# A mixer and expert kernel on one core: down weights in 8 KB pieces, rows scattered by index, gate and up biases on VectorE

## What is computed

```python
def moe(h, w_router, b_router, w_gu, b_gu, w_down, b_down):
    logits = (xt @ w_router + b_router).astype(jnp.float32)
    top_vals, top_idx = lax.top_k(logits, TOP_K)            # 4 of 32
    weights = jax.nn.softmax(top_vals, axis=-1)
    ...
    def expert_block(args):
        xblk, e = args
        gu = xblk @ w_gu[e] + b_gu[e]                       # 1024 -> 2048
        gate, up = jnp.split(gu, 2, axis=-1)
        gate = jnp.minimum(gate, SWIGLU_LIMIT)              # 7
        up = jnp.clip(up, -SWIGLU_LIMIT, SWIGLU_LIMIT)
        act = (up + 1.0) * gate * jax.nn.sigmoid(SWIGLU_ALPHA * gate)
        return act @ w_down[e] + b_down[e]                  # 1024 -> 1024
    ...
    y = jnp.zeros((n_tok + 1, D_MODEL), yb.dtype).at[buf_tok].add(yb * buf_w[:, None])
```

## Time and profile before

| what | value |
|---|---|
| median of 3 runs | 2313.23 us (2310.96 to 2314.2) |
| the profiled execution | 2310.52 us, of which the span (first to last instruction) is 2308.7 us |
| granted TensorE clock, mean | 0.984 |
| busy: PE, DVE, ACT, POOL | 2204.4 us (95%), 795.9 us (34%), 473.4 us (21%), 155.8 us (7%) |
| moved by DMA | 557.15 MB in 145856 packets, mean 241 GB/s |
| of which q1 (issued by SP), q0 (POOL), q10 (ACT) | 513.33 MB, 30.31 MB, 12.67 MB |

### The profile page before, as it was taken

The page is one execution under the profiler, slowest core; times in us unless marked ns, Lnnn a source line. Parts: engine busy times, 40 slices in busy tenths (PEclk is TensorE's granted clock), DMA queues, the critical chain, the costliest instruction groups (busy, mean ns, idle before and its releaser), DMA issues. The chain is left out here.

```text
span 2308.7 us, 35748 instructions
## 1 busy us (share of the span) xinstructions
PE 2204.4 (95%) x14480; PEld 906.0 (39%) x14480; DVE 795.9 (34%) x1427; ACT 473.4 (21%) x848; POOL 155.8 (7%) x186
## 2 busy tenths in 40 slices
PE   5999887999999999999999995999999998999998
PEld 2434442333333333333333334455445444444443
DVE  1132447522222222222222643003176013466543
ACT  2121223111101111011110103010135002545630
POOL 0000002100111001111012311000000000000000
PEclk9999898999999999999999997999999999999999
DMA  9138529999999999999999994121210221122100
GB/s 369 56 114 310 203 107 349 415 417 417 417 416 416 416 417 417 415 416 416 415 417 415 414 406 177 64 73 66 74 54 1 73 73 62 38 91 91 73 37 37
DMA packets 145856, 557.15 MB, mean 241 GB/s; under 512 B 21125, under 2 KB 36654, under 8 KB 111906
## 3 DMA queue, kind: packets, MB, share of 16 engines
q1 hardware_dynamic: 119190, 513.33, 56.1%
q0 software_dynamic: 13200, 30.31, 3.5%
q10 hardware_dynamic: 13404, 12.67, 1.6%
HBM read 545.87 MB, written 25.03 MB: 247 GB/s over the span
## 5 line engine op out<-in xcount | busy, mean ns | idle before, releaser
L1978 PE MATMUL ps<-ring,xeT 128*32 128x512 f32 x6144 | 668.9, 594 | 0.9 <-DVE mT L1768 0.7
L1978 PEld LDWEIGHTS ps<-ring,xeT 128*32 128x32 f32 x6144 | 195.6, 110 | 446.5 <-issue 436.4
L1948 PE MATMUL ps<-ring,mT 128*32 128x512 f32 x2048 | 266.5, 592 | 0.3 <-DMA ring<-in_w_down 0.2
L1701 ACT ACTIVATE mT<-mT 128x768 f32<-128x768 f32 x32 | 27.0, 843 | 867.8 <-DVE mT L1765 867.8
L1765 DVE TENSOR_SCALAR mT<-ps 128x768 f32<-128x768 f32 x32 | 30.6, 958 | 479.9 <-PE ps L1978 479.9
L360 PE MATMUL ps<-hT_late,ring 128*128 128x512 f32 x384 | 165.2, 592 | 1.1 <-ACT hT_late L2230 1.1
L1956 PE MATMUL ps<-ring,mT 128*32 128x256 f32 x2048 | 157.2, 379 | 0.0
L1956 PEld LDWEIGHTS ps<-ring,mT 128*32 128x32 f32 x2048 | 66.2, 110 | 153.5 <-issue 153.5
L2957 PE MATMUL ps<-hT_late,ring 128*128 128x512 f32 x256 | 110.6, 592 | 1.6 <-PEq L2716 1.6
L360 PE MATMUL ps<-ring,mT 128*128 128x512 f32 x256 | 110.1, 592 | 1.2 <-PEq L2521 1.2
L2970 PE MATMUL ps<-hT_late,ring 128*128 128x512 f32 x256 | 110.5, 592 | 0.0
(11 more groups left out here) (407 smaller groups left out, 2070.6 us busy)
## 6 DMA issues: line engine op xcount, KB each, us to landing
ring<-in_w_gu SPq DMA_DIRECT2D x256, 1024.0 KB, 10.6
ring<-in_w_down SPq DMA_DIRECT2D x128, 1024.0 KB, 10.5
ring<-in_even_w_in SPq DMA_DIRECT2D x18, 1024.0 KB, 5.2
ring<-in_w_ada SPq DMA_DIRECT2D x32, 512.0 KB, 6.4
ring<-in_odd_w_in SPq DMA_DIRECT2D x32, 512.0 KB, 5.4
ring<-in_w_ada SPq DMA_DIRECT2D x8, 1024.0 KB, 19.2
ring<-in_w_in SPq DMA_DIRECT2D x8, 1024.0 KB, 15.1
y_scratch<-ysb ACTq DMA_DIRECT2D x128, 64.0 KB
```

The source lines that it names most:

```text
L1701: nc.scalar.activation(sig[:, 0:W], gate[:, 0:W], ACT.Sigmoid, scale=1.702).then_inc(M.sig_ready, 1)
L1948: mm = nc.tensor.matmul(quad(b, 2 * q + n), acted(k, q, src), w[:, kk, n * BANK:(n + 1) * BANK], start=first, stop=last)
L1978: mm = nc.tensor.matmul(quad(q, c), left(q), part_columns(w, c), start=start, stop=stop)
```

## The change

It does these things:

- A piece of `w_down` is now laid out so that partition p gets rows 2p and 2p + 1, which lie side by side: one run of 8 KB in place of two of 4 KB. The features of the activation must then come in another order, which `part_columns` makes: each column part takes every second column, in runs of 32, of the `w_gu` piece. The moving operand of each `gate_up` matmul steps by 8 bytes within a run instead of 4.
- The bias matmuls, `sel` in the loop and the three bfloat16 parts go. `b_gu` is transposed once by 16 small matmuls (behind the first `pe_ids`) and kept per feature in `bT`; each expert's 16 values per partition are copied (`dve_own_bias`) and spread by a transpose of 512 elements (`dve_spread_bias`), and VectorE adds them as it takes gate and up out of PSUM. The limits move: one tensor_scalar for up (with the 1 of up + 1 in the bias), gate's in the product, and the sigmoid's as a limit on its result.
- For the rows of experts 0 to 26, POOL issues two scatters by index (halves and quarters of rows) that leave out the places without a token; ACT issues no stores for them. For the last five experts ACT stores as before.
- Rows that nobody writes must be zero, so the fill covers all of `y_scratch` (53 x 96 rows, 20.8 MB in place of 8.3) and moves to the first block, behind `mod_ready`.

```diff
@@ -289,7 +291,7 @@
                 if j < 8:
                     add(w_gu[e, j * P:(j + 1) * P, :], 2 * FF)
                 else:
-                    add(ktiles(w_down[e], 2 * (j - 8), 2, 0, D), 2, D)
+                    add(w_down[e, (j - 8) * 2 * P:(j - 7) * 2 * P, :].rearrange("(p k) n -> p k n", k=2), 2, D)
...
@@ -564,6 +568,14 @@
                 scol_zeroed.on(nc.gpsimd.memset(scol[:], 0.0))
                 rows_loads.on(pool.dma_start(res[:], A["x"][0].rearrange("(t p) n -> p t n", p=P)), 16)
                 rows_loads.on(pool.dma_start(xc[:], A["ctx"][0].rearrange("(t p) n -> p t n", p=P)), 16)
+
+                scol_zeroed.on(nc.gpsimd.memset(zeros[:], 0.0))
+                scol_zeroed.wait(pool)
+                pool.wait_ge(mod_ready.sem, 3)
+                rows_zeroed.on(pool.dma_start(
+                    y_dram.rearrange("r (h n) -> (r h) n", n=BANK).rearrange("(p a) n -> p a n", p=CAP),
+                    zeros[0:CAP, :].unsqueeze(1).to_broadcast([CAP, (E + XB) * D // BANK, BANK])), 16)
+                rows_zeroed.wait(pool)
 
             @block.scalar
...
-                amat_zero.on(nc.gpsimd.memset(zeros[:], 0.0))
-                amat_zero.wait(pool)
-
-                rows_zeroed.on(pool.dma_start(
-                    y_dram[E * CAP:, :].rearrange("r (h n) -> (r h) n", n=BANK).rearrange("(p a) n -> p a n", p=CAP),
-                    zeros[0:CAP, :].unsqueeze(1).to_broadcast([CAP, XB * D // BANK, BANK])), 16)
-                rows_zeroed.wait(pool)
 
...
         def dve_sel(dve, S, column):
-            nc.vector.tensor_scalar(sel[:], ones[0:3 * E, :], column, None, ALU.mult).then_inc(S.sel_ready, 1)
+            nc.vector.tensor_scalar(sel[:], ones[0:E, :], column, None, ALU.mult).then_inc(S.sel_ready, 1)
+
+        def dve_own_bias(at):
+            nc.vector.tensor_copy(own_bias[:], bT[:, at]).then_inc(bias_spread.sem, 1)
+
+        def dve_spread_bias(dve, e):
+
+            dve.wait_ge(bias_spread.sem, e * 2 + 1)
+            nc.vector.transpose(spread_bias[:], own_bias[:].unsqueeze(2).to_broadcast([P, 16, QUAD]))                 .then_inc(bias_spread.sem, 1)
...
         def part_columns(w, c):
-            return w.rearrange("p (b j c f) -> p c b j f", b=2, c=4, f=QUAD)[:, c]
+            return w.rearrange("p (j c f r) -> p c j r f", c=4, f=QUAD, r=2)[:, c]
...
-                            src = w_down[i + ahead, (j - 8) * 2 * P:(j - 7) * 2 * P, :].rearrange("(k p) n -> p k n", p=P)
+                            src = w_down[i + ahead, (j - 8) * 2 * P:(j - 7) * 2 * P, :].rearrange("(p k) n -> p k n", k=2)
...
-                def block_step(e):
+                def block_step(e, marked):
                     pool.wait_ge(M.ids_read, e + 3)
                     pool.wait_ge(M.xT_done, e + 2)
-                    pass_on(pool, M, e + 1)
+                    pass_on(pool, M, marked)
                     pool_gather(pool, M)
 
-                block_step(0)
-                with pool.Fori(0, E - 4) as i:
-                    block_step(i + 1)
+                def store(e):
+
+                    pool.wait_ge(M.y_read, e + 1)
+                    pass_on(pool, M, e * 2 + 1)
+                    for n, src in enumerate((ysb[:, 0:BANK], ysb[:, Q2])):
+                        nc.gpsimd.indirect_dma_start(
+                            y_parts[n], bass.IndirectOffsetOnAxis(ap=y_idx[:, n:n + 1], axis=0), src, None,
+                            bounds_check=(2 + 2 * n) * E * CAP - 1, oob_is_err=False).then_inc(y_scattered, 16)
+
+                block_step(0, 1)
+                with pool.Fori(0, E - 5) as i:
+                    block_step(i + 1, i * 2 + 2)
+                    store(i + 1)
+                block_step(E - 4, 2 * E - 8)
...
-                parted.on(nc.scalar.copy(bparts[third], bgu[third]))
-                parted.on(nc.scalar.copy(bparts[second], bgu[second]))
-                act.wait_ge(rest.sem, 3)
-                parted.on(nc.scalar.copy(bparts[third], bgu[third]))
...
+                act.wait_ge(bias_turned.sem, 1)
+                by_expert = lambda ap, b: ap.rearrange("p (e g) -> p g e", g=16)[:, 8 * b:8 * b + 8]
+                turned_bias = ps[:, 7, :].rearrange("p (g e) -> p g e", e=E)
+                bias_turned.on(nc.scalar.activation(by_expert(bT[:], 0), turned_bias[:, 0:8], ACT.Copy))
+                bias_turned.on(nc.scalar.activation(by_expert(bT[:], 1), turned_bias[:, 8:16], ACT.Identity, bias=1.0))
...
-                block_step(0, True)
-                with act.Fori(0, E - 2) as i:
-                    block_step(i + 1, False)
+                block_step(0, True, rows=False)
+                with act.Fori(0, SCATTERED) as i:
+                    block_step(i + 1, False, rows=False)
...
+                def block_step(e, first, last=False, between=None, scattered=False, second=False):
                     dve.wait_ge(M.gate_done, e + 1)
-                    nc.vector.tensor_scalar(thirds(gate), part_banks(0), 7.0, None, ALU.min).then_inc(M.gu_read, 1)
+                    dve.wait_ge(bias_spread.sem, e * 2 + 2)
+                    bias = [spread_bias[:, b * FQ:(b + 1) * FQ].unsqueeze(1).to_broadcast([P, 3, FQ]) for b in range(2)]
+                    nc.vector.tensor_tensor(thirds(gate), part_banks(0), bias[0], ALU.add).then_inc(M.gu_read, 1)
                     if not first:
                         dve.wait_ge(M.aT_read, e)
-                    nc.vector.tensor_scalar(thirds(up), part_banks(1), 7.0, -7.0, ALU.min, ALU.max).then_inc(M.gu_read, 1)
+                    nc.vector.tensor_tensor(thirds(up), part_banks(1), bias[1], ALU.add).then_inc(M.gu_read, 1)
                     if not last:
-                        dve_sel(dve, M, ident3[:, e + 1:e + 2] if isinstance(e, int) else ident3[:, bass.ds(e + 1, 1)])
+                        dve_own_bias(bass.ds((e + 1) * 16, 16))
                     dve.wait_ge(M.gu_read, e * 2 + 2)
-                    nc.vector.scalar_tensor_tensor(out=up[:, 0:W], in0=up[:, 0:W], scalar=1.0, in1=gate[:, 0:W], op0=ALU.add,
+
+                    nc.vector.tensor_scalar(up[:, 0:W], up[:, 0:W], 8.0, -6.0, ALU.min, ALU.max).then_inc(M.ug_ready, 1)
+                    if not last:
+                        dve_spread_bias(dve, e + 1)
+                    dve.wait_ge(M.ug_ready, e * 2 + 1)
+                    nc.vector.scalar_tensor_tensor(out=up[:, 0:W], in0=gate[:, 0:W], scalar=7.0, in1=up[:, 0:W], op0=ALU.min,
                                                    op1=ALU.mult).then_inc(M.ug_ready, 1)
-                    dve.wait_ge(M.ug_ready, e + 1)
+                    dve.wait_ge(M.ug_ready, e * 2 + 2)
                     dve.wait_ge(M.sig_ready, e + 1)
-                    nc.vector.tensor_tensor(up[:, 0:W], up[:, 0:W], sig[:, 0:W], ALU.mult).then_inc(M.act_ready, 1)
+                    nc.vector.scalar_tensor_tensor(out=up[:, 0:W], in0=sig[:, 0:W], scalar=SIG7, in1=up[:, 0:W], op0=ALU.min,
+                                                   op1=ALU.mult).then_inc(M.act_ready, 1)
                     dve.wait_ge(M.act_ready, e + 1)
...
-                        read_y(e, Y0)
-
-                def read_y(e, b):
-
-                    dve.wait_ge(M.y_stored, e * 128)
+                        read_y(e, Y0, scattered, not second)
+
+                def read_y(e, b, scattered=False, after_first=True):
+
+                    if scattered:
+                        if after_first:
+                            dve.wait_ge(y_scattered, e * 32 - 32)
+                        nc.vector.tensor_copy(y_idx[:], y_places[:, :, bass.ds(e - 1, 1)].rearrange("p n e -> p (n e)"))
+                    else:
+                        rows_stored(dve, e - 1)
...
                 prepare(0)
+                dve.wait_ge(bias_turned.sem, 3)
+                dve_own_bias(slice(0, 16))
+                dve_spread_bias(dve, 0)
...
+                experts = cst[:, C_IOTA32:C_IOTA32 + E]
+                for n in range(2):
+                    col = C_Y + 2 * n
+                    step(nc.vector.tensor_scalar(tmp32, count, cst[:, col:col + 1], float(16 * NONE), ALU.is_le, ALU.mult))
+                    step(nc.vector.scalar_tensor_tensor(out=tmp32, in0=experts, scalar=float((2 + 2 * n) * CAP), in1=tmp32,
+                                                        op0=ALU.mult, op1=ALU.add))
+                    step(nc.vector.tensor_scalar(y_places[:, n, :], tmp32, cst[:, col + 1:col + 2], None, ALU.add))
...
+                    if e == 0:
+                        bgu_loaded.wait(pe)
+                        for g in range(16):
+                            mm = nc.tensor.transpose(ps[:, 7, g * E:(g + 1) * E],
+                                                     bgu[:, (g // 2) * 2 * P:(g // 2 + 1) * 2 * P].rearrange(
+                                                         "e (p r) -> e r p", r=2)[:, g % 2], ident[0:E, 0:E])
+                        bias_turned.on(mm)
...
```

(49 more changed lines are left out.)

53 lines of the change are left out of this document (24 added, 29 removed).

## The result

| | before | after |
|---|---|---|
| median of 4 runs | 2312.79 us (2310.96 to 2314.20) | 2328.65 us (2326.99 to 2329.75) |
| ratio, 95% interval | | 1.0066 [1.0053, 1.0079] |
| span of the profiled execution | 2308.7 us | 2327.1 us |

A forecast was written before the change was run, and what follows sets the result against it. PE was taken to set the loop's pace, the DMA nearly full; 32 x 0.65 = 20.8 us less, all else nothing: 2310.5 - 20.8 = 2289.7, the runs' median 2.7 above, so 2292.5 us; range 2286 to 2304.

The forecast's parts named there:

- PE's turn without the bias matmuls: Experts' loop: dropping the bias group takes 0.65 us off each of 32 turns, 20.8 us; a turn becomes 31.25 us.
- I take nothing, since the rows nearest to it show four groups at full pace with a pattern that is already broken.: Gate and up's moving operand: the 8-byte step costs nothing; upper bound twice the 20.63 us.
- a rival with its place, L2040: Gate and up, 96 matmuls a turn: the 8-byte step slows them, deciding from 3%; at full bound 2952 us; 12%.
- The rule beside it: Gate and up's reads: hitting a 16-byte line at least twice keeps full speed, so an 8-byte step costs nothing.
- Together 31.90 - 0.3 - 0.4 = 31.2 us, just under PE's 31.25.: DMA need per loop turn: 8 KB pieces save 0.3 us, scatters 0.4, so the DMA can follow PE.
- the DMA rival: Loop: scatters cost what the stores did, DMA needs 31.6 us a turn, gain only 9.6 us, 2303.6 us; 12%.
- it moves forward by as much as PE does: Behind the loop: the DMA saves 20.7 us in sum, so the DMA-bound end moves forward and waits stay about the same.
- Zeros: Fill in the first block: 12.5 MB more, all 20.8 MB take 50 us, cost nothing; at worst 30 us.
- start: Before the first expert: DVE comes free some 6 us earlier, the 16 transposes lie where PE is idle; nothing.
- scatters on POOL: Loop: two scatters delay the next gathers by up to 2 x 1.3 us, with over 20 us to spare.
- VectorE: Loop: at most 2.2 us a turn of new work on 8.1 of 31.25, covered; uncovered, 2 us a turn would show.
- What I said would show it: Signs: turns of 31.25 us if right; gate and up over 20.7 us (step) or mid-loop DMA ring waits if wrong.

The follow-up runs named there:

- e9: e1 with SP issuing all eight stores of the last experts' rows ahead of the even_w_in loads; 2309.26 us, ratio 0.9985.
- e11: e9 with the eight stores ahead of dft_c and fourier_w too; 2305.14 us, ratio 0.9963.
- e12: e1 with only the first four of SP's eight stores ahead of the even_w_in loads, the others behind; 2302.37 us, ratio 0.9957.
- e1: The changed kernel without the 8-byte step: runs of 64 floats, VectorE's transposes make the feature order; 2304.73 us, ratio 0.9959.
- e5: The kernel before, with gate and up's moving operand taking each fourth float32, 16 bytes apart; 3021.52 us (one run).
- e6: The kernel before, with steps elsewhere: down's 512-column matmuls and first-block projections 8 bytes, late k/v projection 16; 4072.03 us (one run), extra expert blocks ran.
- e2: The kernel before, with gate and up's moving operand taking each second float32 (8-byte step); 2344.27 us, ratio 1.0123.
- e10: The kernel before, with a step of 8 bytes in down's 256-column matmuls alone; 2312.11 us (one run).
- e3: e1 with w_down in 4 KB rows and features in natural order; 2314.20 us, ratio 1.0003.
- e7: e1 with 4 KB w_down rows, natural feature order and ACT's stores instead of scatters; biases on VectorE and the early fill stay; 2316.12 us, ratio 1.0020.
- e4: e1 with ACT's eight stores for all experts in place of the scatters; 2304.35 us, ratio 0.9967.

## Why the prediction was wrong

**PE's turn without the bias matmuls**: right, in the terms. 31.25 was forecast; 31.24 is what each kernel without the bias matmuls and without a step shows, e9, e11 and e12 with their gap apart.

**"I take nothing, since the rows nearest to it show four groups at full pace with a pattern that is already broken."** This step failed. Runs of 32 with gaps are another thing than a step inside a run: e1's runs of 64 go at 0.43 us for four, the step of 8 bytes at 0.4535. I had this as a rival with its place, L2040, and the point from which it decides, 3%. It was 5.5%: 1.14 us a turn where the sum had nothing, and 23.9 us of the whole (2328.65 for e1's 2304.73). Its chance should have been far above 12%: a resource at 100%, a price that no row shows, and 192 instructions a turn on it, so that a twentieth of a row ate the gain. The rival's time, 2952 us, was its upper bound; measured was an eighteenth of the 20.63 us and not all of it.

**The rule beside it.** The Trainium skill (Advanced Engine Details and Errata, SBUF Cachelines) wants two hits on a 16-byte line for full speed. At 16 bytes, one hit, the time is 2.10 times as long (e5), which agrees in its direction. At 8 bytes, two hits, it is not quite full speed: 5% less, with one column group as with four. The measurement decides here.

**"Together 31.90 - 0.3 - 0.4 = 31.2 us, just under PE's 31.25."** Wrong too, and hidden by the step. 8 KB pieces were worth 0.2 to 0.3 as said; the scatters 0.1 to 0.2 and not 0.4, where I had taken a saving in the packets' busy time for a saving of the loads. The need was 31.56 us, which is the DMA rival (31.6, 2303.6 us): without the step the kernel takes 2304.7. Its form was another: the turns don't lengthen, the lag gathers in the ring and comes out at the end. The step "it moves forward by as much as PE does" fell with it: in e1 the end costs 10.5 us in two turns and 2.4 us behind them. So I had two rivals, and both happened; a sum over alternatives didn't have that case.

**Zeros, start, scatters on POOL, VectorE**: right in that nothing is paid. DVE's busy time went from 8.1 to 9.2 us a turn, and POOL's from 3.2 to 5.5, with no PE wait for either in the loop. The landing of the fill was off by a factor of two, 100.3 us for 50, without effect, so that "nothing" was right here by the room that there was and not by the estimate.

**What I said would show it**: gate and up over 20.7 us for the step. The first timeline above has it, 21.77 us.

## What to carry to other kernels

When PE is full, a new access pattern of the moving operand is the first thing to price, by one matmul group with it: here 5.5% on the widest group cost 23.9 us, and the rest of the change gave 9.0. A reordering is better put into a pass of an engine with time to spare, here VectorE's transpose. When two resources are both full, taking work off one gives nothing until the other is relieved as well, and with a deep ring the loss doesn't show in the turns: read the drift of the landing times, not the turn.

## What the runs showed of the hardware

- A moving operand of float32 read with a step of 8 bytes takes 5% longer (0.450 for 0.429 us per 512 columns, 128x128 weights, e6) or 5.5 to 5.8% (four 32-column groups, the changed kernel and e2); four of 256 columns pay 0.010 us (e10) where four of 512 pay 0.024. With 16 bytes it takes 2.10 times as long (0.900 us in e6, 0.90 in e5). Runs of 32 or 64 floats side by side with gaps between cost nothing (0.43 us for four, as down's runs of 512).
- VectorE's transposes with a step of 8 bytes in their source keep their 0.98 us for 768 elements (979 ns in e1, 978 in the earlier trace rows).
- Loads of `w_down` in rows of 8 KB and not 4 KB gave 9.5 to 11.8 us of the whole in kernels whose DMA is the bound (e3 to e1, e7 to e4).
- While the DMA was behind, one issue of a 1 MB load took 16.05 us on SP (e1).
- A turn of the same PE program was 31.24 us (e1) or typically 31.77 to 31.91 us, the latter in the three kernels whose SP program was changed behind the loop. The cause stays open.
